# Feed-forwards that open token-major, a ring of ten weight units, and loads moved to the SyncE queue

## The chip, the cores and the metric

The kernel runs on one core of a Trainium2 chip. The metric is the device time of one execution in microseconds; the time before is the median of three executions. PE is TensorE, ACT ScalarE, DVE VectorE, POOL GpSimd, SP SyncE.

## The reference

Three transformer blocks run one after the other over 256 tokens of width 1024, and everything is float32. What matters here is the shape of one block:

```
h = h + rms_norm(mixer(rms_norm(h, n0)), n1)
h = h + rms_norm(ffn(rms_norm(h, n2)), n3)
conv_ffn: u, v = split(y @ w_up);  c = b + sum_j conv_w[j] * shift(u, j);  (gelu(c) * v) @ w_down
```

Block 0 has the even mixer (window attention and a gated recurrence), block 1 the odd mixer (attention with relative bias, 16 heads). The third block has three attention branches, one norm ahead of them and one ahead of its feed-forward, silu(gate) * up in place of the convolution, and no norm behind its products. The hidden width of a feed-forward is 2816, that is 22 column tiles of 128 features. Each column tile of a feed-forward has two halves: u (or gate) and v (or up).

## The kernel before, in words

**Split precision.** Each float32 operand is used as a rounded part `hi` and a rest `lo`; a product is three matmuls (hi·hi, hi·lo, lo·hi). Weights arrive as 346 *units* of 128x1024 floats (512 KB). SP loads a unit into slot n % 8 of `raw` as soon as the unit eight before it is used (`unit_used`, L399). ACT rounds it (`hi<-raw`, L500), DVE subtracts (`lo<-raw,hi`, L1148), PE waits for `lo_done`. ACT and DVE execute in program order, so the calls `units(upto)` between the other steps say when units are rounded and split.

**Two ways to multiply.** *Token-major* (`tokens_by`, matmuls on L788): 128 tokens of the activations are the stationary operand, 512 weight columns move; a unit holds 128 rows of the weights, and it takes six matmuls for each of the two token tiles. I call these six a *part*. *Feature-major* (`features_of`, L852): 128x128 weights are stationary and both token tiles move (256 columns); a unit holds all 1024 rows of 128 columns and takes 24 matmuls. It needs both token tiles of the activations from its first matmul on. The up-projection of each feed-forward is feature-major (44 units, `each_tile`, which is straight code for the first four tiles, a loop for sixteen, and straight code for two), and the down-projection is token-major (22 units).

**What stands between a projection and the next one.** The last `TAIL` = 6 units of a projection that ends in a norm run as a group: token tile 0 of all six, then token tile 1 of all six, so that tile 0 is normed while PE works on tile 1. `norms_between` (L540 on ACT, L1216 on DVE) does for each token tile: sum of squares of the product (ACT, L520), times gain (`weigh_product`, L1179), the root (POOL, L428 and L430), add into `h` (L1212), squares and gain again for the next norm (L520, L1179), root, `scale` (L1193). Then PE transposes the tile (`turn_normed`, eight transposes on L863), ACT copies the rounded part (`turned_hi`, L538) and DVE the rest (`turned_lo`, L1199). The transposes of tile 0 are put ahead of the last unit's part of tile 1 (L817). Those of tile 1 stand ahead of what follows: in a feed-forward ahead of its first matmul (`turn_normed(stage, base, 1)`, L1018), in a token-major projection ahead of the sixth unit of the leading group of six (`LEAD`, L809), which runs tile 0 first. There are five such boundaries between two projections: even_out to up0, down0 to odd_v, odd_out to up1, down1 to moba_qk, and merge_out to up2 (this one has no norm on the product). In the three that lead to an up-projection (`FEATURE_MAJOR`) no weight unit is split between the two products with the gain and `scale` of tile 1; in the other two, one is split ahead of `scale` and one behind it.

**Other loads.** POOL issues the gain rows (512 KB each, broadcast), twelve constants and sixteen bias tables from its own queue. SP issues the input `h`, the memory input and the weights.

Of the kernel before, what the change touches and what calls it, by code (L numbers as in the profile page):

```python
# [45 lines left out]
RAW = 8  # L46
# [5 lines left out]
    ("up0", 44, 8, 128), ("down0", 22, 1, 1024),  # L52
    ("odd_v", 8, 1, 1024), ("odd_qk", 16, 8, 128), ("odd_out", 8, 1, 1024),
    ("up1", 44, 8, 128), ("down1", 22, 1, 1024),
    ("moba_qk", 8, 1, 1024), ("both_v", 8, 1, 1024), ("fox_qk", 8, 1, 1024), ("mem_q", 8, 1, 520),
    ("gates", 24, 8, 128), ("branches", 12, 4, 256), ("merge_out", 8, 1, 1024),
    ("up2", 44, 8, 128), ("down2", 22, 1, 1024),
# [18 lines left out]
LEAD, TAIL = 6, 6  # L76
# [51 lines left out]
def lay_out(a):  # L128
# [8 lines left out]

    r = np.arange
# [6 lines left out]
    u += columns(a["ffn_w_up"][0], two) + rows(a["ffn_w_down"][0], r(D))  # L145
    u += rows(odd, r(2048, 3072)) + columns(odd, pairs) + rows(a["odd_w_out"][0], r(D))
    u += columns(a["ffn_w_up"][1], two) + rows(a["ffn_w_down"][1], r(D))
# [5 lines left out]
    u += columns(np.concatenate([a["w_gate_2"][0], a["w_up_2"][0]], 1), two) + rows(a["w_down_2"][0], r(D))  # L153
# [22 lines left out]
def build(nc, dram, out):  # L176
    with ExitStack() as ctx:
# [52 lines left out]
        nlf = sb("nlf", [NT, P])  # L230
# [48 lines left out]
        state = [s.rearrange("p (h e) -> p h e", h=HB) for s in state]  # L279
        qc_t = xhat[:, 0, :].rearrange("p (a b) -> p a b", a=4)  # L280
# [27 lines left out]
        conv_begun, conv_done, glued = sem("conv_begun"), sem("conv_done"), sem("glued")  # L308
        hmul, h_hi_done, h_lo_done = sem("hmul"), sem("h_hi_done"), sem("h_lo_done")
# [44 lines left out]
        def each_tile(engine, tile):  # L354

            for r in range(4):
                tile(0, r)
            with engine.Fori(1, KF // 4) as i:
                for r in range(4):
                    tile(i, r)  # L360
            for r in range(KF % 4):
                tile(KF // 4, r)

        def qk_place(j, f):

            if j == 0:
                return ps[:, 2 + f, 0:S]
            return ps[:, 6 + f, S * (j % 2):S * (j % 2) + S]

# [17 lines left out]
        def _(sp):  # L387

            sp.dma_start(mem_x[:, 0, :], dram["mem"][0:P, :]).then_inc(mem_in[0], 16)
            sp.dma_start(ident[:, :], dram["c_ident"]).then_inc(ident_in, 16)  # L390
            for n in range(RAW):
# [4 lines left out]
                sp.dma_start(raw[:, n, :], dram["weights"][n]).then_inc(raw_in[n], 16)  # L396
            with sp.Fori(0, UNITS // RAW - 1) as i:
                for s in range(RAW):
                    sp.wait_ge(unit_used, RAW * i + s + 1)  # L399
                    sp.dma_start(raw[:, s, :], dram["weights"][RAW * i + (RAW + s)]).then_inc(raw_in[s], 16)  # L400
            for n in range(UNITS - UNITS % RAW, UNITS):
                sp.wait_ge(unit_used, n - RAW + 1)
                sp.dma_start(raw[:, n % RAW, :], dram["weights"][n]).then_inc(raw_in[n % RAW], 16)
# [6 lines left out]
        def _(pool):  # L410
            def gain_load(g):
                if g >= 2:
                    pool.wait_ge(weighed, half_count(g - 2, 1, 1))
                pool.dma_start(gain[:, g % 2, :], dram["gains"][g:g + 1, :].partition_broadcast(P)).then_inc(gain_in[g % 2], 16)

            pool.memset(half[:, :], -0.5).then_inc(set_up, 1)
            gain_load(0)
            gain_load(1)
# [13 lines left out]
            def head_roots(i, nh, d):  # L432
# [7 lines left out]
            loads = [  # L440
                (rope_a[:, :, :, :].rearrange("p a t f -> p (a t f)"), dram["c_rope_a"]),
                (rope_m[:, :, :, :].rearrange("p a t f -> p (a t f)"), dram["c_rope_m"]),
                (window[:, :], dram["c_window"]), (causal[:, :], dram["c_causal"]),
                (block_causal[:, :], dram["c_block"]), (keep[:, :], dram["c_keep"]),
                (pick[:, :, :].rearrange("p a b -> p (a b)"), dram["c_pick"]),
                (conv[:, :, :, :].rearrange("p a b c -> p (a b c)"), dram["conv"]),
                (head_gain[:, :], dram["head_gains"].partition_broadcast(P)),
                (rows_in[:, :], dram["rows_in"].partition_broadcast(P)),
                (lb_in[:, :, :].rearrange("p a b -> p (a b)"), dram["lb"]),
                (hw[:, :], dram["hgrn_w"].partition_broadcast(P)),  # L450
            ]
            for dst, src in loads:
                pool.dma_start(dst, src).then_inc(const_in, 16)
            pool.memset(ones[:, :], 1.0).then_inc(set_up, 1)
            pool.memset(s_t[:, :, :, :], 0.0).then_inc(set_up, 1)
            pool.memset(nlf[:, :, :], 0.0).then_inc(set_up, 1)
            gain_load(2)
            gain_load(3)
# [10 lines left out]
            gain_load(4)  # L469
            gain_load(5)  # L470
            root(4, 5)
            gain_load(6)
            gain_load(7)

            pool.wait_ge(unit_used, last("down0"))
            for hh in range(16):
                if hh >= 4:
                    pool.wait_ge(row_max, ATT["c"][0] + hh - 3)
                pool.dma_start(bias[:, hh % 4, :], dram["rel"][hh]).then_inc(bias_in[hh % 4], 16)
            root(6, 7)  # L480
            gain_load(8)
            gain_load(9)
            root(8, 9)
            gain_load(10)
# [7 lines left out]
        def _(act):  # L492
            done = [0]

            def round_unit(n, s=None, q=None, w=None):

                s, q = (n % RAW, n // RAW) if s is None else (s, q)
                act.wait_ge(raw_in[s], 16 * (q + 1))
                w = WIDTH[n] if w is None else w
                act.activation(hi[:, s, :w], raw[:, s, :w], ACT.Copy).then_inc(hi_done, 1)  # L500

            def units(upto):
                loops = (upto - done[0]) // RAW
                if loops >= 2:
                    n = done[0]
                    with act.Fori(0, loops) as i:
                        for s in range(RAW):
                            round_unit(RAW * i + (n + s), (n + s) % RAW, i + (n + s) // RAW, UNIT)
                    done[0] += RAW * loops
# [30 lines left out]
            def norms_between(g, p, base, name, stage, turn_base):  # L540


                units(last(name) + 2)
# [8 lines left out]
                if stage not in FEATURE_MAJOR:  # L552
                    units(last(name) + 6)
# [18 lines left out]
            def feed_forward(layer):  # L572

                up = FIRST[f"up{layer}"]
                J0 = KF * layer

                def copy(j, r):
                    act.wait_ge(hmul, J0 + j + 1)
                    act.activation(h_hi[:, j, :], pt[:, r % 2, :S], ACT.Copy).then_inc(h_hi_done, 1)

                def tile(i, r):

                    j = 4 * i + r
                    n, m = 8 * i + (up + 2 * r), up + 2 * r + 4
                    act.wait_ge(unit_used, n + 2)
                    if layer < 2:
                        act.activation(sc[:, r % 2, :S], ps[:, r, :S], ACT.Identity, scale=conv[:, layer, j, 2:3],  # L587
# [1034 lines left out]
```

## Time and profile before

| | |
|---|---|
| time, median of 3 (lowest, highest) | 1190.43 us (1188.77, 1191.32) |
| the profiled execution's own time | 1188.9 us |
| its span, first to last instruction | 1187.1 us |
| PE busy | 1125.4 us, 95% |
| DVE, ACT, POOL busy | 714.5, 560.1, 76.4 us |
| mean granted clock of PE | 0.959 |
| the chain that ended last | PE 88%, DVE 4%, ACT 3%, DMA 2% |

A matmul row such as `286 ns` is longer than the distance to the next one, since matmuls are pipelined; the distance between starts is what a matmul costs. In a timeline row the first number is the start, the second the time that the merged instructions cover, and a bracket holds the idle time of that engine just before it and what ended it.

### The profile page before, as it was taken

Reading aid. Unit: us, or ns where it says so; the run is one execution under the profiler, and the core shown is the slowest. Engines: PE = TensorE matmul, PEld = TensorE weight load, DVE = VectorE, ACT = ScalarE, POOL = GpSimd, SP = SyncE. Lnnn points to the kernel's source line nnn. Section 1 sums busy time; section 2 is a strip of 40 time slices with the busy share of each in tenths; the row PEclk is TensorE's granted clock in tenths of the full one; section 3 lists DMA queues with packets and bytes.
Section 4 is the critical chain, followed back from the end, with each engine's and each line's share of the span. In section 5 each row is a group of like instructions: output and inputs, shape, how many; then the busy total and the mean of one; then the engine's idle time right before and its main releaser. Section 6 shows DMA issues by size and latency. Waiting matters only on the chain.

```text
span 1187.1 us, 19769 instructions
## 1 busy us (share of the span) xinstructions
PE 1125.4 (95%) x7452; PEld 1022.4 (86%) x7452; DVE 714.5 (60%) x1111; ACT 560.1 (47%) x917; POOL 76.4 (6%) x113
## 2 busy tenths in 40 slices
PE   5999996999999899869999998999999997999998
PEld 4898676999988799759999886888999987999986
DVE  5668445666664656555666646756555675555552
ACT  5544333555553454434555534446543733444541
POOL 3300001000000211010000001212000000000000
PEclk9999578999999999889999999999999998999999
DMA  7953014545554653145554544665333344545552
GB/s 292 309 192 123 1 36 164 190 179 177 189 189 155 239 168 143 66 163 160 179 188 182 185 170 159 230 199 175 110 107 108 147 143 156 190 178 179 190 191 77
DMA packets 53934, 195.24 MB, mean 164 GB/s; under 512 B 6272, under 2 KB 6464, under 8 KB 53872
## 3 DMA queue, kind: packets, MB, share of 16 engines
q1 hardware_dynamic: 50816, 184.64, 45.2%
q0 software_dynamic: 3056, 9.73, 2.5%
q8 instruction: 45, 0.74, 0.2%
q14 instruction: 17, 0.14, 0.1%
HBM read 193.29 MB, written 1.05 MB: 164 GB/s over the span
## 4 chain that ended last, share of the span: by engine, by line
PE 88%; DVE 4%; ACT 3%; DMA 2%; POOL 1%; issue 1%; SPq 0%; ACTq 0%; DVEq 0%
PE ps L852 46%; PE ps L788 31%; PE ps L936 3%; PE ps L913 3%; DMA raw<-in_weights 2%; DVE lo L1148 2%; PE ps L925 1%; PE ps L863 1%; ACT hi L500 1%; DVE y_lo L1199 1%; ACT pr L520 1%; POOL ms L428 1%; PE ps L882 1%; PE ps L990 0%; POOL rstd L430 0%
## 5 line engine op out<-in xcount | busy, mean ns | idle before, releaser
L1148 DVE TENSOR_TENSOR lo<-raw,hi 128x1024 fp32r<-128x1024 f32 (+2 forms) x346 | 409.7, 1204 | 115.1 <-ACT hi L500 114.3
L852 PE MATMUL ps<-y_hi,hi 128*128 128x256 f32 x1504 | 430.8, 286 | 2.0 <-DVE y_lo L1199 2.0
L852 PE MATMUL ps<-y_lo,hi 128*128 128x256 f32 x1504 | 428.1, 285 | 0.0
L852 PE MATMUL ps<-y_hi,lo 128*128 128x256 f32 x1504 | 428.0, 285 | 0.0
L500 ACT ACTIVATE hi<-raw 128x1024 fp32r<-128x1024 f32 (+2 forms) x346 | 350.2, 1036 | 123.3 <-DMA raw<-in_weights 115.5
L852 PEld LDWEIGHTS ps<-y_hi,hi 128*128 128x128 f32 x1504 | 291.1, 194 | 4.1 <-issue 3.7
L852 PEld LDWEIGHTS ps<-y_lo,hi 128*128 128x128 f32 x1504 | 291.1, 194 | 0.0
L852 PEld LDWEIGHTS ps<-y_hi,lo 128*128 128x128 f32 x1504 | 290.9, 193 | 0.0
L788 PE MATMUL ps<-hi,h_hi 128*128 128x512 f32 x328 | 102.8, 395 | 3.9 <-DVE h_lo L1199 2.5
L788 PE MATMUL ps<-hi,h_lo 128*128 128x512 f32 x328 | 102.5, 394 | 0.0
L788 PE MATMUL ps<-lo,h_hi 128*128 128x512 f32 x328 | 102.2, 393 | 0.0
L788 PE MATMUL ps<-hi,y_hi 128*128 128x512 f32 (+2 forms) x288 | 87.9, 386 | 6.1 <-DVE y_lo L1199 3.6
L788 PE MATMUL ps<-lo,y_hi 128*128 128x512 f32 (+2 forms) x288 | 86.3, 380 | 0.0
L788 PE MATMUL ps<-hi,y_lo 128*128 128x512 f32 (+2 forms) x288 | 86.2, 380 | 0.0
L587 ACT ACTIVATE sc<-ps,conv 128x256 f32<-128x256 f32 x44 | 24.8, 565 | 121.2 <-PE ps L852 121.2
L788 PEld LDWEIGHTS ps<-hi,h_hi 128*128 128x128 f32 x328 | 61.1, 189 | 18.2 <-DVE h_lo L1199 2.9
L788 PEld LDWEIGHTS ps<-hi,h_lo 128*128 128x128 f32 x328 | 61.9, 189 | 13.6
L1317 DVE SCALAR_TENSOR_TENSOR sc<-ps,conv,sc 128x255 f32<-128x255 f32 x44 | 21.2, 483 | 86.9 <-ACT sc L587 86.9
L788 PEld LDWEIGHTS ps<-lo,h_hi 128*128 128x128 f32 x328 | 61.9, 189 | 13.2
L788 PEld LDWEIGHTS ps<-hi,y_hi 128*128 128x128 f32 x288 | 52.8, 191 | 17.9 <-DVE y_lo L1199 5.3
L788 PEld LDWEIGHTS ps<-lo,y_hi 128*128 128x128 f32 x288 | 53.7, 190 | 10.5
L788 PEld LDWEIGHTS ps<-hi,y_lo 128*128 128x128 f32 x288 | 53.5, 190 | 10.5
(237 smaller groups left out, 974.1 us busy)
## 6 DMA issues: line engine op xcount, KB each, us to landing
raw<-in_weights SPq DMA_DIRECT2D x346, 512.0 KB, 3.5
gain<-in_gains POOLq DMA_DIRECT2D x11, 512.0 KB, 5.3
bias<-in_rel POOLq DMA_DIRECT2D x16, 128.0 KB, 2.9
mem_x<-in_mem SPq DMA_DIRECT2D x2, 512.0 KB, 7.1
h<-in_x SPq DMA_DIRECT2D x1, 1024.0 KB, 14.0
out<-h SPq DMA_DIRECT2D x2, 512.0 KB, 2.6
pick<-in_c_pick POOLq DMA_DIRECT2D x1, 512.0 KB, 6.0
head_gain<-in_head_gains POOLq DMA_DIRECT2D x1, 256.0 KB, 6.7
```

The costliest lines, as they stand in the source:

```text
L428: pool.tensor_scalar(ms[:, g % 2, t:t + 1], ss[:, g % 2, t, 0:1], ss[:, g % 2, t, 1:2], EPS, ALU.add, ALU.add).then_inc(scaled_ms, 1)
L500: act.activation(hi[:, s, :w], raw[:, s, :w], ACT.Copy).then_inc(hi_done, 1)
L520: act.activation(junk[t][:, i, :], halves[i], ACT.Square, scale=D ** -0.5, accum_out=ss[:, g % 2, t, i:i + 1]).then_inc(squared, 1)
L587: act.activation(sc[:, r % 2, :S], ps[:, r, :S], ACT.Identity, scale=conv[:, layer, j, 2:3], bias=conv[:, layer, j, 3:4]).then_inc(conv_be ...
L788: mm = pe.matmul(ps[:, base + 2 * t + half_, :cw], x[:, k, tok], w[:, n % RAW, c0:c0 + cw], start=first and k == 0, stop=final and n == la ...
L852: mm = pe.matmul(dst, w[:, s % RAW, at], x(k), start=first and k == 0, stop=final and k == nk - 1)
L863: mm = pe.transpose(ps[:, base + 2 * t + kh, kk * P:(kk + 1) * P], src[:, t, (4 * kh + kk) * P:(4 * kh + kk + 1) * P], ident[:, :])
L882: mm = pe.transpose(ps[:, b, kk * P:(kk + 1) * P], src[:, t, c0 + kk * P:c0 + (kk + 1) * P], ident[:, :])
L913: mm = pe.matmul(dst, q[:, t * P:(t + 1) * P], k[:, :n], start=True, stop=stage != "f")
L936: mm = pe.matmul(place(stage, hh, t), pt[:, a % 2, i * P:(i + 1) * P], v(kt), start=kt == 0, stop=kt == kts[-1])
L1148: dve.tensor_tensor(lo[:, s, :w], raw[:, s, :w], hi[:, s, :w].bitcast(F32), ALU.subtract).then_inc(lo_done, 1)
L1317: dve.scalar_tensor_tensor(c[:, 1:S], ps[:, r, 0:S - 1], conv[:, layer, j, 1:2], c[:, 1:S], ALU.mult, ALU.add).then_inc(dve_link, 1)
```

## The change

- The ring has ten slots (`RAW` 8 to 10). The groups at projection ends have seven units (`TAIL` 6 to 7). Three units of the next projection are split ahead of the first norm, where there were two. One of them is split ahead of `turned_lo` of tile 0, where there were two; one between that and the product of tile 1 with the gain; one ahead of `scale` of tile 1, now in all five boundaries. The transposes of tile 0 stand one part earlier.
- A feed-forward's first three column tiles (`lead0` to `lead2`, six half units each: 512 rows by 256 columns) are made token-major, all of token tile 0, then all of token tile 1. The transposes of token tile 1 of the activations stand ahead of the sixth half unit of token tile 0. The result is copied to `xhat` and turned to feature-major by twelve transposes, behind the first half of the fourth column tile.
- All loads are issued by SP, in one program order with the weights: gain 0 ahead of the first weights, gain 1 behind `x`, constants two at a time ahead of units 10 to 15, the other gains and the bias tables at fixed places. POOL issues none.
- No loops are left in the program of any engine. `nlf` lies in a part of `gate`; its memset on POOL stands later.

```diff
-RAW = 8
+RAW = 10
-LEAD, TAIL = 6, 6
+LEAD, TAIL, LEADS = 6, 7, 3
...
+        def ahead(j):
+            return 11 + j if j < 4 else 2 * j + 7
...
@@ SP
+            GAIN_AT = {FIRST["even_qf"]: (2, 3), FIRST["up0"] + 10: (4, 5), FIRST["odd_qk"] + 4: (6, 7), FIRST["up1"] + 10: (8, 9),
+                       FIRST["both_v"] + 6: (10,)}
+            gain_load(0)
+            for n in range(UNITS):
...
+                for g in GAIN_AT.get(n, ()):
+                    gain_load(g)
+                if n >= RAW:
+                    sp.wait_ge(unit_used, n - RAW + 1)
+                    for dst, src in loads[2 * (n - RAW):2 * (n - RAW) + 2]:
+                        sp.dma_start(dst, src).then_inc(const_in, 16)
+                for hh in BIAS_AT.get(n, ()):
+                    bias_load(hh)
+                sp.dma_start(raw[:, n % RAW, :], dram["weights"][n]).then_inc(raw_in[n % RAW], 16)
@@ ACT, feed_forward
+                act.wait_ge(lead_made, 2 * layer + 1)
+                act.activation(xhat[:, 0, 0:512], bank(0), ACT.Copy).then_inc(lead_copied, 1)
+                act.wait_ge(lead_made, 2 * layer + 2)
+                act.activation(xhat[:, 0, 512:768], lead_place(2, 0), ACT.Copy).then_inc(lead_copied, 1)
+                units(up + 10)
+                act.wait_ge(unit_used, up + 4)
+                act.activation(xhat[:, 1, 0:512], bank(2), ACT.Copy).then_inc(lead_copied, 1)
@@ PE
-                        if is_tail and n == last(name) - 1:
+                        if is_tail and n == last(name) - 2:
                             turn_next()
...
+                def lead(t):
+                    for j in range(LEADS):
+                        for half_ in range(2):
...
+                            if j == 0:
+                                pe.wait_ge(y_lo_done, 4 * stage + 2 * t + half_ + 1)
+                            if t == 0 and n == up + 2 * LEADS - 1:
+                                turn_normed(stage, base, 1)
+                            for kk in range(4):
+                                k, c = 4 * half_ + kk, slice(256 * kk, 256 * kk + 256)
+                                for x, w in ((y_hi, hi), (y_hi, lo), (y_lo, hi)):
+                                    mm = pe.matmul(lead_place(j, t), x[:, k, tok], w[:, n % RAW, c], ...)
...
+                lead(0)
+                lead(1)
+                column(3, 0)
+                pe.wait_ge(lead_copied, 4 * layer + 4)
+                for j in range(LEADS):
+                    turn_lead(j)
+                column(3, 1)
+                for j in range(4, KF):
+                    if j >= 8:
+                        pe.wait_ge(hmul, KF * layer + j - 3)
+                    column(j, 0)
+                    column(j, 1)
@@ DVE, norms_between
-                units(last(name) + 2)
+                units(last(name) + RAW - TAIL)
                 weigh_product(g, 0, base, tile_done, TAILS.index(name) + 1)
...
                 units(last(name) + 4)
                 turned_lo(stage, turn_base, y_lo, y_hi, (0,))
+                units(last(name) + 5)
                 weigh_product(g, 1, base, unit_used, last(name))
                 add_product(g, p, 1)
                 weigh(g + 1, 1, [h[:, 1, 0:512], h[:, 1, 512:D]])
-                if stage not in FEATURE_MAJOR:
-                    units(last(name) + 5)
+                units(last(name) + 6)
                 scale(g + 1, 1)
@@ DVE, feed_forward
+                units(up + 10)
+                dve.wait_ge(unit_used, up + 6)
+                dve.tensor_copy(xhat[:, 1, 512:768], lead_place(2, 1)).then_inc(lead_copied, 1)
+                for j in range(KF):
...
+                    units(up + ahead(j) - 1)
                     dve.wait_ge(glued, J0 + j + 1)
...
+                    units(up + ahead(j))
```

## Rows read from the trace of the kernel before

**Rows 1.** The page: granted clock and traffic in 40 slices of the span.
```profile
PEclk9999578999999999889999999999999998999999
...
GB/s 292 309 192 123 1 36 164 190 179 177 189 189 155 239 168 143 66 163 160 179 188 182 185 170 159 230 199 175 110 107 108 147 143 156 190 178 179 190 191 77
```

**Rows 2.** Who PE waited for over the span: us, times, longest.
```profile
PE ps L863 <- DVE xhat L1193: 33.5, 4, 10.4
...
PE ps L788 <- DVE lo L1148: 3.3, 3, 1.3
```

**Rows 3.** Busy time by stretch: length, PE, PEld, DVE, ACT, POOL, clock, DMA share, GB/s.
```profile
187.10:198.00 10.90, 2.05 (x9) 1.68 (x9) 7.09 (x13) 4.02 (x11) 3.17 (x6) 0.72 0.44 134
198.00:202.00 4.00, 4.00 (x19) 4.00 (x20) 0.61 (x1) 0.00 (x0) 0.00 (x0) 0.50 0.41 166
...
520.60:532.00 11.40, 1.99 (x9) 1.62 (x9) 7.59 (x13) 4.47 (x12) 3.17 (x6) 0.60 0.39 124
532.00:536.00 4.00, 4.00 (x19) 4.00 (x20) 0.69 (x1) 0.00 (x0) 0.00 (x0) 0.50 0.36 147
...
985.10:993.70 8.60, 2.04 (x9) 1.67 (x9) 6.48 (x11) 4.42 (x8) 1.13 (x2) 0.62 0.36 138
993.70:997.30 3.60, 3.60 (x17) 3.60 (x18) 0.64 (x1) 0.00 (x0) 0.00 (x0) 0.50 0.02 7
```

**Rows 4.** Timeline at the boundary from even_out to up0.
```profile
177.82 1.40 DVE L1179 TENSOR_TENSOR xhat<-ps,gain 128x512 f32<-128x512 f32 x2
...
186.46 0.63 PE L788 MATMUL ps<-hi,y_lo 128*128 128x512 f32 x2
...
187.36 1.28 DVE L1199 TENSOR_TENSOR y_lo<-ps,y_hi 128x512 fp32r<-128x512 f32 x2
...
188.56 1.28 DVE L1179 TENSOR_TENSOR xhat<-ps,gain 128x512 f32<-128x512 f32 x2
...
192.61 1.29 DVE L1179 TENSOR_TENSOR xhat<-h,gain 128x512 f32<-128x512 f32 x2
...
193.49 0.58 POOL L428 TENSOR_SCALAR ms<-ss 128x1 f32<-128x1 f32 x1 [2.43 <-ACT pr L520]
...
194.75 0.88 DVE L1193 TENSOR_SCALAR xhat<-xhat,rstd 128x512 f32<-128x512 f32 x2 [0.84 <-POOL rstd L430]
...
195.29 1.97 PE L863 MATMUL ps<-ident,xhat 128*128 128x128 f32 x8 [8.21 <-DVE xhat L1193]
```

**Rows 5.** Timeline at the boundary from down0 to odd_v.
```profile
389.53 0.73 PE L788 MATMUL ps<-hi,y_hi 128*128 128x512 f32 x2 [1.32 <-DVE y_lo L1199]
...
394.92 1.63 POOL L428 TENSOR_SCALAR ms<-ss 128x1 f32<-128x1 f32 x1 [2.43 <-ACT pr L520]
...
396.52 0.73 PE L788 MATMUL ps<-hi,y_hi 128*128 128x512 f32 x2 [1.26 <-DVE lo L1148]
...
399.30 1.09 PE L863 MATMUL ps<-ident,xhat 128*128 128x128 f32 x8 [1.12 <-DVE lo L1148]
```

**Rows 6.** The chain that ended last: start, us, what.
```profile
165.46 14.99 PE ps L788 x66
...
820.66 5.76 PE ps L852 x48
```

**Rows 7.** Timeline of the start, and of DVE near 46 us.
```profile
8.59 1.29 DVE L1179 TENSOR_TENSOR xhat<-mem_x,gain 128x512 f32<-128x512 f32 x2 [8.59 <-DMA gain<-in_gains]
...
14.84 1.22 PE L788 MATMUL ps<-hi,h_hi 128*128 128x512 f32 x2 [2.48 <-DVE h_lo L1199]
...
45.91 0.68 DVE L1245 TENSOR_REDUCE hs<-sc 128x4 f32<-128x512 f32 x1
```

**Rows 8.** Timeline of one column tile of up0 on ACT and DVE.
```profile
223.65 0.48 DVE L1317 SCALAR_TENSOR_TENSOR sc<-ps,conv,sc 128x255 f32<-128x255 f32 x1 [1.82 <-ACT sc L587]
...
224.77 0.40 ACT L594 ACTIVATE pr<-sc 128x256 f32<-128x256 f32 x1
224.90 1.22 DVE L1148 TENSOR_TENSOR lo<-raw,hi 128x1024 fp32r<-128x1024 f32 x1
```

More of the change, by code:

```diff
@@ L136, in columns, with up @@
         return [w[:, cols[c:c + width]].reshape(-1, P, width).transpose(1, 0, 2).reshape(P, -1) for c in range(0, len(cols), width)]
+    def up(w):
+        first = [x[:, c:c + UNIT] for x in columns(w, two[:LEADS * 256], 256) for c in (0, UNIT)]
+        return first + columns(w, two[LEADS * 256:])
     r = np.arange
@@ L352, in build @@
         junk = [sc, pr]
[L354 to L362, printed above, removed]
         def qk_place(j, f):
@@ L468, in _ @@
             root(2, 3)
-            gain_load(4)
-            gain_load(5)
             root(4, 5)
[L472 to L479, printed above, removed]
             root(6, 7)
-            gain_load(8)
-            gain_load(9)
+            pool.memset(nlf, 0.0).then_inc(set_up, 1)
             root(8, 9)
-            gain_load(10)
             for i in (4, 5, 6, 7):
@@ L493, in _, with round_unit @@
             done = [0]
[L495 to L499, printed above, removed]
+            def round_unit(n):
+                s, w = n % RAW, WIDTH[n]
+                act.wait_ge(raw_in[s], 16 * (n // RAW + 1))
                 act.activation(hi[:, s, :w], raw[:, s, :w], ACT.Copy).then_inc(hi_done, 1)
             def units(upto):
[L503 to L509, printed above, removed]
                 while done[0] < upto:
@@ L1029, in feed_forward @@
-                each_tile(pe, tile)
+                up = FIRST[f"lead{layer}"]
+                def lead(t):
+                    tok = slice(t * P, (t + 1) * P)
+                    for j in range(LEADS):
+                        for half_ in range(2):
+                            n = up + 2 * j + half_
+                            if t == 0:
+                                wait_unit(n)
+                            if j == 0:
[5 more added lines that the diff above has]
+                                for x, w in ((y_hi, hi), (y_hi, lo), (y_lo, hi)):
+                                    mm = pe.matmul(lead_place(j, t), x[:, k, tok], w[:, n % RAW, c],
+                                                   start=k == 0 and x is y_hi and w is hi, stop=k == KD - 1 and x is y_lo)
+                            if t == 1:
+                                mm.then_inc(unit_used, 1)
+                        if t == 0 and j >= 1:
+                            mm.then_inc(lead_made, 1)
@@ new lines, in turn_lead, with column @@
+                def turn_lead(j):
+                    for f in range(2):
+                        for t in range(NT):
+                            mm = pe.transpose(up_place(j, f)[:, t * P:(t + 1) * P], xhat[:, t, 256 * j + P * f:256 * j + P * f + P], ident[:, :])
+                    mm.then_inc(lead_turned, 1)
+                def column(j, f):
+                    n = up + 2 * j + f
+                    features_of(n, n % RAW, [up_place(j, f)], of_tiles(Y)).then_inc(unit_used, 1)
+                lead(0)
@@ L1224, in norms_between @@
                 turned_lo(stage, turn_base, y_lo, y_hi, (0,))
+                units(last(name) + 5)
                 weigh_product(g, 1, base, unit_used, last(name))
@@ L1589, in _ @@
             merged_low(1)
-            units(last("merge_out"))
+            units(last("merge_out") + RAW - TAIL)
             add_residual("merge_out", 4, 0)
```

185 lines of the change are left out of this document (77 added, 108 removed).

## The prediction, made before the changed kernel ran

> **What bounds the kernel now.** I read the page first: PE is busy for 95% of the span and carries the chain that ended last, so only what PE stands still for, or runs at a low clock for, can be won. [rows 1] show the clock lowest in the fifth to seventh slice (118 to 208 us) and dips at the 17th, 18th and 34th. Then the waits of PE: 33.5 us in four waits go to the normed activations, of which the longest, 10.4 us, is the start of the kernel [rows 2]. The other three, 23.1 us, are the openings of the three feed-forwards. The windows put numbers on them: the stretches from the last matmul of a projection to the first of the up-projection are 10.9, 11.4 and 8.6 us, with some 2 us of PE work in each (eight transposes), and behind each PE runs at clock 0.50, the level of 1.2 GHz, for 4.0, 4.0 and 3.6 us [rows 3]. The timeline says why: up0 needs both token tiles, and the norm of tile 1 can't begin before the last part of even_out [rows 4]. The opening of the token-major odd_v, which has tile 0 to work on, loses only 1.32, 1.26 and 1.12 us [rows 5].
>
> **Units used below.** A part (six token-major matmuls) takes 14.99 / 11 = 1.36 us; a feature-major matmul takes 5.76 / 48 = 0.12 us [rows 6], so one token tile of a lead half unit (12 matmuls of 256 columns) takes 1.44 us. I take the 256-column form in either layout as the same price: both load 128x128 and move 256 columns, and there are 24 for a unit before and after. A transpose takes 1.09 / 8 = 0.136 us at full clock [rows 5].
>
> **Feed-forward openings: what goes.** Stretches of 10.9 + 11.4 + 8.6 = 30.9 us. At full clock the 19, 19 and 17 matmuls behind them would take 2.28, 2.28 and 2.04 us, so the low clock costs 1.72 + 1.72 + 1.56 = 5.0 us. Together 35.9 us.
>
> **What comes back.** (1) The eight transposes of tile 1: 3 x 1.09 = 3.3 us. (2) Twelve transposes of the lead: 12 x 0.136 = 1.64 us, three times 4.9 us. Ends: 1.09 x 12/8 as taken, and at low clock 1.97 x 12/8 = 2.96 us each [rows 4], which would add 4.0 us; I take the first, as PE doesn't stand still ahead of them. (3) A rest of the wait for tile 1. Call E the end of the last part. For E, tile 0 must be turned: its chain takes from the product's end (177.82) until about 184.6 us, five parts, before and after the change, and y_lo of tile 0, now with one split (1.2 us) ahead of it instead of two and one part more of cover, is ready about 1 us before E; it was 1.5 us late (187.36 + 1.28 = 188.64 against E = 186.46 + 0.63 = 187.09). DVE then splits one unit and is free at E + 0.2. The chain of tile 1 runs 188.56 to 193.90 (5.34 us) up to the end of the second product with the gain; `scale` began 0.85 us later [rows 4]. Now a split stands between them. Where one stands there already, at odd_v, POOL's first root instruction took 1.63 us [rows 5] instead of 0.58 [rows 4], 1.05 us more, and `scale` waits for it: 0.85 + 1.05 = 1.9 us after the product. So the first normed half is there at E + 0.2 + 5.34 + 1.9 + 0.44 = E + 7.9. PE has five half units of lead until its transposes: 5 x 1.44 = 7.2 us. The wait is 0.7 us, twice 1.4 us. At up2 there is no norm on the product, the chain is shorter by over 2 us, and I take none. Ends for each opening: 0, and 2 us if DVE starts the chain as late as before (1.3 us more). Behind the transposes the sixth half unit (1.44 us) covers the copy of half a tile (about 0.6 + 0.7 us), so `lead(1)` waits for nothing.
>
> On the same rows, the Trainium skill, "SBUF — State Buffer", section "Who interferes with whom", says that a VectorE instruction with two inputs in SBUF keeps out a GpSimd instruction that reads SBUF. The split has two, and the trace agrees: 1.63 us with a split beside it, 0.58 without. It speaks against the change, since the split now stands there in the feed-forward boundaries as well. By it the wait is the 0.7 us above; without it `scale` would wait for the split alone and there would be nearly none.
>
> Net for the three: 35.9 - 3.3 - 4.9 - 1.4 = 26.3 us.
>
> **Openings of odd_v and moba_qk.** The wait for y_lo of tile 0 (1.32) goes, as above. The fifth unit's split now stands ahead of the tile-1 chain, so the wait for it (1.26) goes. What is late next is `scale`: PE reaches the transposes at E + 5 x 1.36 = 6.8 against E + 7.9, 1.1 us. So 3.70 becomes 1.1, and with the second, which repeats the pattern (the waits for the split in [rows 2] are three, two of them these), 5.2 us go. Ends: 1.4 (only the first wait goes each time, and half of that) and 7.4.
>
> **Start.** The first norm waited for gain 0 until 8.59 [rows 7], while gain 1 was moving beside it; now gain 1 comes behind `x`. At the 300 GB/s of the first slices [rows 1] a 512 KB load takes 1.7 us. In the one queue, gain 0 should land near 6.3, units 0 and 1 near 8.0 and 9.7; rounding, the copy of tile 0 and its rest put the first matmul near 12.8 instead of 14.84 [rows 7]. I take 1.9 us. Ends: 3, and -3 if `x` and gain 1 come late for the second norm. The constants come in the weights' queue up to unit 15. Adding up 12.9 MB at 300 to 320 GB/s they are complete near 43 to 45 us, and DVE wants them at 45.91 - 1.9 = 44.0 [rows 7]: 0 to 3 us of wait with little cover behind it, I take 0.5. Net 1.4 us.
>
> **The first tiles of the up-projections.** Behind the turned lead, tiles 0 to 3 get one split each. For a tile, DVE's cycle is from its first convolution step (223.65) to gelu's end (225.17), 1.52 us, then rounding 1.05, the split 1.22: about 3.8 us [rows 8]. The 15th unit is then split some 21 us after the first turned tile, with the table load of gelu (1.3 us) in it, and PE wants it 21.2 us after. So it just holds; I take 0.4 us in all, ends 0 and 3 us for each of two layers. Later tiles have two splits in about 4.2 us of DVE against 5.8 us of PE, so they catch up. Units 6 to 9 of an opening are split in the 9 us in which PE does `lead(1)`, and land before that at one unit in 1.7 to 2.3 us. The four copies of the lead are covered by `lead(1)` and the half column behind it (2.9 us).
>
> **Priced at nothing.** Groups of seven: no work is added, but PE comes to each unit of the group one part (1.36 us) earlier. In the down-projections the splits run ahead by the ring's depth, which hides it. In merge_out and odd_out, of eight units, the last four or two are split while PE works on the first; if that cover is gone it costs up to one split, 1.2 us, at each. I take none. Gains and bias tables in SP's order: each wait there is for something that is over when its turn comes, with nine units (over 25 us) queued ahead of the weights held back. Straight code instead of loops: the gates stage is straight code and does 48 matmuls in 5.76 us [rows 6], 0.1200 us each, and the loops run at the same within 0.001 us; over 2304 matmuls this is 0 to 2.3 us. POOL loses its DMA issues, which nobody waited for.
>
> **Sum.** 26.3 + 5.2 + 1.4 - 0.4 = 32.5 us. Against the profiled execution's 1188.9 us this is 1156.4; its time is 1.5 us under the median shown, so for the median 1158 us.
>
> **Rivals.**
> - *The openings are hidden, but the weights or the vector engine are late behind them* (15%): the 3.8 us cycle of the first four tiles is the thin place. At 4.5 us a tile it costs 4 x 0.7 = 2.8 us in layers 0 and 1, and with the start's gain lost as well, 2.8 x 2 + 1.4 = 7: 1165 us. For it: the margin is a few tenths. Against: DVE is idle for 1.82 us in each tile now [rows 8].
> - *Tile 1 isn't covered and the clock falls again* (8%): if the tile-1 chain starts late, PE waits 2 to 3 us at all five openings and the clock drops at the three feed-forwards (5.0 us): about 15 us back, 1173 us. Against: at odd_v waits of 1.3 us left the clock at full level.
> - *The change doesn't do what it says* (3%): lead(0) can't start before both tiles, because y_lo of tile 0 or the fourth and fifth units come with tile 1. Then 35.9 us stay and only the 5 us of the token-major openings and the start are left, less 4.9 us of transposes: 1189 us.
> - *Slower* (4%): fetching straight code. The loops of the up-projections hold 16 of 22 tiles; unrolled, 3 x 16 x 48 = 2304 matmuls and as many weight loads stream through PE's sequencer once each. From 32.5 / 2304 = 14 ns a matmul on (0.134 instead of 0.120 us) the gain is gone; at 20 ns, 1204 us. Against: the straight stages of the same density above. The Trainium skill, "Runtime: NRT & Kernel Launch", section "Instruction fetch mechanics", has it the other way round: a taken branch can stall the fetch, and straight code is preferred. By it there would be a gain here; the trace shows none to be had, as PE had no idle time in the loops.
>
> **How the numbers follow.** The forecast case has 70%, its own range is 1152 to 1163 us (the low end is all waits at nothing and 3 us at the start). To leave out no more than 2 in 10, the range reaches into the first rival: 1151 to 1168 us. Under 0.2% (2.4 us) a measurement of this kernel can't tell a change from none. Faster 0.94, same 0.02, slower 0.04.
>
> **What would show it.** Right: no wait of PE for the normed activations above 1.5 us after the start of the kernel, clock 1.00 over all openings, first matmul of the lead within 0.3 us of the group's end, twelve transposes in about 1.6 us, first matmul of the kernel near 12.8 us. Wrong: waits for `lo` in tiles 5 to 8 of an up-projection, a wait of DVE for constants over 3 us, gaps in long runs of matmuls that no semaphore explains, or a clock of 0.5 behind a boundary.

## The result, and the profile after

| | median us (lowest to highest, executions) | ratio to before, 95% |
|---|---|---|
| before, measured beside it | 1190.32 (1188.77 to 1191.32, 4) | |
| after | 1153.76 (1152.48 to 1154.90, 4) | 0.9696 [0.9683, 0.9709] |

36.6 us faster; forecast were 1158 and a range of 1151 to 1168. The two profiled executions are 1188.9 and 1154.57 us (spans 1187.1 and 1152.8), 34.3 apart, against a sum of 32.5. The other 2.2 us are where these two executions happened to lie in their own spreads: 1.4 under the median before, 0.8 over it after.

The page's slices of the granted clock and of the traffic, after:

```profile
PEclk9999569999999999899999999999999999999999
GB/s 326 313 194 146 1 19 139 259 184 182 185 186 150 214 208 151 79 133 245 184 183 184 192 135 206 229 213 148 129 102 103 145 130 215 186 184 184 187 193 37
```

The dips behind the three feed-forward boundaries are gone from the clock [rows 1]; those of the attention stages (fifth, sixth and seventeenth slice) stay. The waits of PE after, in total us, times, longest:

```profile
PE ps L859 <- DVE xhat L1213: 14.1, 5, 10.3
PE ps L784 <- DVE lo L1175: 1.6, 1, 1.6
PE ps L859 <- DVE y_lo L1219: 1.1, 2, 0.6
```

Before, 33.5 us in four waits [rows 2]. Now 10.3 are the start and 3.8 are shared by the four openings that have a product norm. No wait for `lo` is left but one at the start. Windows after, with PE busy first and its clock in the column behind POOL, of up0's opening, of the up-projection behind it, and of the openings of odd_v and moba_qk:

```profile
188.00:192.00 4.00, 4.00 (x36) 4.00 (x35) 2.73 (x5) 2.91 (x8) 0.86 (x2) 1.00 0.72 239
192.00:201.00 9.00, 8.25 (x71) 8.08 (x70) 5.88 (x9) 5.00 (x9) 2.19 (x2) 1.00 0.07 11
201.00:317.40 116.40, 116.40 (x973) 116.40 (x972) 79.85 (x124) 62.78 (x103) 0.00 (x0) 1.00 0.61 203
376.00:388.00 12.00, 10.87 (x54) 8.83 (x53) 8.96 (x13) 5.99 (x14) 3.06 (x4) 1.00 0.48 168
696.40:708.20 11.80, 10.68 (x52) 8.68 (x51) 8.86 (x13) 5.79 (x13) 3.06 (x4) 1.00 0.49 182
```

Where the windows of before had 2 us of PE work in 10.9 us and then clock 0.50 [rows 3], PE is now busy for all but 0.75 us of 188 to 201, at clock 1.00, and then without a gap for 116.4 us. The timeline of the same opening (start, us covered), the last part of even_out, the first lead matmul, and the chain of tile 1, to be laid beside [rows 4]:

```profile
186.95 0.61 PE L784 MATMUL ps<-hi,y_lo 128*128 128x512 f32 x2
187.41 0.28 PE L1028 MATMUL ps<-hi,y_hi 128*128 128x256 f32 x1
187.62 1.46 DVE L1199 TENSOR_TENSOR xhat<-ps,gain 128x512 f32<-128x512 f32 x2
...
189.19 0.30 POOL L461 TENSOR_SCALAR ms<-ss 128x1 f32<-128x1 f32 x1 [6.05 <-ACT pr L517]
...
192.56 1.63 POOL L461 TENSOR_SCALAR ms<-ss 128x1 f32<-128x1 f32 x1 [2.43 <-ACT pr L517]
192.89 1.22 DVE L1175 TENSOR_TENSOR lo<-raw,hi 128x1024 fp32r<-128x1024 f32 x1
194.28 0.56 POOL L463 TENSOR_TENSOR rstd<-ms,half 128x1 f32<-128x1 f32 x1
194.87 0.88 DVE L1213 TENSOR_SCALAR xhat<-xhat,rstd 128x512 f32<-128x512 f32 x2 [0.76 <-POOL rstd L463]
195.50 1.06 PE L859 MATMUL ps<-ident,xhat 128*128 128x128 f32 x8 [0.75 <-DVE xhat L1213]
```

The lead follows the last part without a gap, and POOL's root instruction takes 1.63 us beside the split. At 189.19 the same instruction takes 0.30 us, with DVE idle. So the 0.58 us of [rows 4] is more than its price alone: its first 0.4 us lie beside DVE's product with the gain. The chain that ended last, from there (start, us):

```profile
196.57 10.07 PE ps L1028 x84
206.64 2.88 PE ps L848 x24
209.52 1.31 PE ps L1038 x12
```

84 lead matmuls in 10.07 us are 0.1199 each, the price of the feature-major form [rows 6]; twelve transposes hold PE for 1.31 us. At up2, where no norm lies on the product, both turns stand in unbroken work:

```profile
955.34 0.87 PE ps L859 x8
956.21 2.75 PE ps L784 x12
958.97 7.20 PE ps L1028 x60
966.17 0.87 PE ps L859 x8
967.04 10.07 PE ps L1028 x84
```

### The profile page after: what moved, and what is told of

It is laid out like the page before. It is cut to its first block, busy times and chain, and to the rows that moved or that the text cites. A ratio compares the mean times of both kernels' runs of the same rounds, so it can differ in the third digit from the quotient of the medians.

```text
span 1152.8 us, 18024 instructions
## 1 busy us (share of the span) xinstructions
PE 1119.6 (97%) x7488; PEld 1020.2 (89%) x7488; DVE 716.0 (62%) x1114; ACT 558.5 (48%) x926; POOL 57.4 (5%) x74
## 4 chain that ended last, share of the span: by engine, by line
PE 90%; ACT 3%; DVE 3%; POOL 2%; issue 1%; DMA 1%; SPq 0%; ACTq 0%; DVEq 0%
PE ps L848 42%; PE ps L784 33%; PE ps L1028 3%; PE ps L932 3%; PE ps L909 3%; PE ps L859 2%; PE ps L921 2%; ACT pr L517 1%; POOL ms L461 1%; DVE lo L1175 1%; DMA raw<-in_weights 1%; POOL rstd L463 1%; PE ps L878 1%; ACT hi L504 1%; PE ps L986 1%
## 5 line engine op out<-in xcount | busy, mean ns | idle before, releaser
L848 PE MATMUL ps<-y_hi,hi 128*128 128x256 f32 x1360 | 387.2, 285 | 0.0
L848 PE MATMUL ps<-y_hi,lo 128*128 128x256 f32 x1360 | 384.8, 283 | 0.0
L848 PE MATMUL ps<-y_lo,hi 128*128 128x256 f32 x1360 | 384.8, 283 | 0.0
L504 ACT ACTIVATE hi<-raw 128x1024 fp32r<-128x1024 f32 (+2 forms) x346 | 346.5, 1036 | 76.4 <-DMA raw<-in_weights 76.2
L848 PEld LDWEIGHTS ps<-y_hi,hi 128*128 128x128 f32 x1360 | 260.7, 192 | 1.0 <-issue 0.7
L848 PEld LDWEIGHTS ps<-y_lo,hi 128*128 128x128 f32 x1360 | 260.7, 192 | 0.0
L848 PEld LDWEIGHTS ps<-y_hi,lo 128*128 128x128 f32 x1360 | 260.7, 192 | 0.0
L564 ACT ACTIVATE pr<-sc,neg 128x128 f32<-128x128 f32 x80 | 35.4, 445 | 49.4 <-DVE neg L1297 49.2
```

The source lines that it names most:

```text
L564: e = act.activation(pr[:, a % 2, c], src, ACT.Exp, bias=neg[:, col, t:t + 1], accum_out=tot[:, col, t:t + 1])
L848: mm = pe.matmul(dst, w[:, s % RAW, at], x(k), start=first and k == 0, stop=final and k == nk - 1)
```

## The experiments

Each edit is one to the kernel after, unless it says otherwise. "Before" of the batches was 1189.7, 1189.4 and 1189.3 us; the medians of different batches are compared only where the gap is several us.

### Which part of the change brings the time

**ring_only**: ring of ten, groups of seven, early turn, the new order of splits and SP's loads, without the lead (all columns feature-major, from the first on; the copies and turns of the lead go with it).

```diff
-("lead0", 6, 4, 256), ("up0", 38, 8, 128)
+("lead0", 0, 4, 256), ("up0", 44, 8, 128)      # lead1, lead2 alike
-LEAD, TAIL, LEADS = 6, 7, 3
+LEAD, TAIL, LEADS = 6, 7, 0
```

> The changed kernel without its token-major lead: the up-projections are feature-major from their first tile, as before; the ring of ten, groups of seven, the early transposes of tile 0 and SP's loads stay. Theory (the lead covers the norm of tile 1): each opening stands still again for the chain of tile 1. It starts some 1.3 us earlier than before and has the split ahead of scale (1.05 us), so the stretches are near 10.6, 10.6 and 7.5 us, with the clock at 0.50 for about 4 us behind each; against the changed kernel 25 us more, 1179 us. Rival (the deeper ring and the earlier transposes bring most of it): under 1165 us, with waits of PE for the normed activations of under 5 us at each feed-forward.

Measured 1178.78 (1178.00 to 1181.02), ratio 0.9915 [0.9889, 0.9941]. Its wait and one of its windows:

```profile
PE ps L852 <- DVE xhat L1201: 33.5, 6, 10.4
```

```profile
197.00:202.00 5.00, 4.75 (x25) 4.78 (x26) 0.80 (x2) 0.24 (x1) 0.00 (x0) 0.57 0.00 0
```

The 33.5 us stay, and so does the low clock behind them. The lead is worth 25 us of the 36.6; the rest of the change alone brings 11. By the starts of the same matmuls in the profiled executions of before and of ring_only, 6.2 of these 11 lie in the openings of odd_v and moba_qk, 2.8 in those of the three feed-forwards, and 1.6 in the odd mixer, where the clock is low for 6.9 us instead of 10.2.

**lead_only**: the lead and SP's loads, with ring, groups and turn as before. `RAW - TAIL` is also the number of units split ahead of the first norm: three after, two here and in ring8_early, four in groups_six.

```diff
-RAW = 10
+RAW = 8
-LEAD, TAIL, LEADS = 6, 7, 3
+LEAD, TAIL, LEADS = 6, 6, 3
-if is_tail and n == last(name) - 2:
+if is_tail and n == last(name) - 1:
```

> The lead kept, but a ring of eight, groups of six and the transposes of tile 0 ahead of the last part, as before. Theory: the lead brings most, and the ring's share is that DVE starts the chain of tile 1 on time: two splits stand ahead of y_lo of tile 0 again, so PE waits 1.3 us for it at an opening, and the tile-1 chain starts about 2.5 us later, some 3.2 us of waits at four openings instead of 0.9; 10 us more than the changed kernel, 1164 us. Rival (with eight slots the weights of the lead are late, as they arrive at one in 1.7 to 2.3 us against 1.44 us of use): waits for lo in every opening and over 1172 us.

Measured 1170.25 (1163.33 to 1172.27), ratio 0.9823 [0.9777, 0.9869]: 6 us above the theory. No opening waits for `lo`, so the rival is false. What came instead is the clock: it fell again behind the waits of odd_v, up1, moba_qk and up2:

```profile
390.90:394.30 3.40, 3.20 (x12) 2.94 (x13) 1.73 (x4) 1.82 (x3) 0.00 (x0) 0.50 0.00 0
524.00:527.40 3.40, 3.40 (x19) 3.40 (x18) 1.29 (x2) 2.06 (x5) 0.00 (x0) 0.50 0.00 0
718.50:721.90 3.40, 3.40 (x13) 2.92 (x12) 1.86 (x3) 2.65 (x4) 0.00 (x0) 0.51 0.00 0
974.50:977.90 3.40, 3.40 (x18) 3.40 (x18) 3.37 (x6) 1.33 (x4) 1.01 (x1) 0.51 0.08 34
```

Four times 3.4 us at half the clock cost up to 6.8 us, the size of the miss. At up0 the clock stayed, with waits of 2.0 us for `xhat` and 0.9 for y_lo, where up1 has 2.0 and 1.4. Its one execution at 1163.3 us, 7 us under the others, had a mean clock of 0.975 against their 0.968 to 0.969; 0.7% of 1168 us is 8 us. That execution has no trace, so that the four drops are what it lacks is inferred from its mean clock. Together with ring_only this shows an interaction: 11 and 19.5 us alone, 36.6 together, 6 more than the sum (which counts twice what both runs share, SP's loads). The trace of after has no such drop, so the clock is large enough for all of the 6; that is argued from sizes, no run separates it.

**turn_late**: the turn of tile 0 one part later.

```diff
-if is_tail and n == last(name) - 2:
+if is_tail and n == last(name) - 1:
```

> Only the place of tile 0's transposes goes back to one part before the end; ring and groups stay. Theory (DVE's order sets the tile-1 chain): y_lo of tile 0 ends 1.4 us later, the split behind it too, the chain of tile 1 starts 1.4 us later, and PE's wait at the transposes of tile 1 grows from 0.8 to 1.1 us to 2.2 to 2.5 us at four openings: 5.5 us more, 1159 us. Rival (there is slack between the two): same time as the changed kernel within 1 us.

Measured 1159.79 (1158.42 to 1162.10), ratio 0.9751 [0.9723, 0.9779]. Its wait row:

```profile
PE ps L859 <- DVE xhat L1213: 19.7, 5, 10.4
```

5.5 us more waiting than after (9.3 against 3.8 without the start), about one part (1.36) at each of four openings, and 6.0 to 6.3 us more time. Tile 0 is turned a part later, so ACT and DVE finish with it a part later and start the chain of tile 1 later: at up0 DVE's product of tile 1 starts at 188.65, 1.6 us behind the group's end at 187.06, where after has 0.2. The four waits are 2.1, 2.5, 2.1 and 2.5 us long. Behind the one at odd_v the clock was 0.51 from 390.2 to 393.7, some 1.7 us of time; behind the other 2.5 us, at moba_qk, and behind the two of 2.1 it stayed at full level.

**groups_six** and **ring8_early** divide the rest.

```diff
-LEAD, TAIL, LEADS = 6, 7, 3
+LEAD, TAIL, LEADS = 6, 6, 3      # groups_six; ring8_early has RAW = 8 besides
```

> After with groups of six instead of seven at the projection ends, ring of ten and all else kept. It divides what lead_only lost between ring and groups. Theory: the group's length is what counts, since it sets how long TensorE works on the second token tile while VectorE weighs and scales the first: one part of a unit (6 matmuls of 0.24, 1.44 us) is missing at each of five ends, less the slack of about 0.75, so 3 to 4 us: 1157 us, and the ring is then worth the other 7. Rival: the ring counts for nothing here, and groups_six comes out as slow as ring8_early, 1162 or more.

> After with the ring of eight half units and groups of six, the turn two parts before the end and everything else of the change kept: the run lead_only with the early turn. Theory: the early turn is worth what turn_late lost, 6.3 us, whatever the ring: 1164 us. What then still lies above after (10.5 us) belongs to ring and groups alone, as waits of TensorE for xhat and y_lo in the openings. Rival: with groups of six the early turn waits for VectorE itself and brings under 2 us: 1168 to 1170.

groups_six: 1160.27 (1158.52 to 1160.93), ratio 0.9753 [0.9740, 0.9766], 6.8 us above the repeat of after (1153.46), twice what I expected. The waits, and the place in question in even_out's group:

```profile
PE ps L859 <- DVE xhat L1213: 20.3, 9, 10.7
```

```profile
186.04 0.88 DVE L1213 TENSOR_SCALAR xhat<-xhat,rstd 128x512 f32<-128x512 f32 x2 [0.86 <-POOL rstd L463]
186.59 1.10 PE L859 MATMUL ps<-ident,xhat 128*128 128x128 f32 x8 [1.44 <-DVE xhat L1213]
```

Nine waits instead of five. The chain over tile 0 runs from 179.81 to the first normed half at 186.48, 6.7 us. Five parts (6.8 us) just cover it, four (5.4) don't: PE stands for 1.44 us ahead of the early turn at each of four ends, 5.8 us, and that is most of the 6.8. I had counted a slack of 0.75 that isn't there.

ring8_early: 1171.38 (1164.92 to 1173.34), ratio 0.9830 [0.9805, 0.9855], where the theory had 1164 and the rival 1168 to 1170. It isn't faster than lead_only (1170.25): with groups of six the early turn waits, as just shown. The fastest execution of each, 1164.92 and 1163.33, says the same. The rival holds: the early turn brings nothing in groups of six. What groups of seven bring without the early turn no run shows. Its chain ahead of tile 1's norm at up0, and the turn at its end:

```profile
182.12 4.62 DMA raw<-in_weights
...
186.76 1.07 ACT hi L504
...
187.85 1.23 DVE lo L1175
189.08 1.20 DVE y_lo L1219 x2
190.28 1.13 DVE lo L1175
191.41 0.61 DVE xhat L1199
```

```profile
199.21 1.06 PE L859 MATMUL ps<-ident,xhat 128*128 128x128 f32 x8 [1.91 <-DVE xhat L1213]
```

A slot that comes free late means a load that lands late (4.62 us from its issue), and its rounding and split stand in DVE's order ahead of y_lo and of tile 1's product. The first lead matmul, which marks the group's end, is at 189.95 here and tile 1's product at 191.33, 1.4 us behind it; after, these are 187.41 and 187.62, 0.2 apart. The 1.2 us come out as wait: 1.91 instead of groups_six's 0.75 at up0, and in all 24.9 us of waits for `xhat` (10.8 at the start) against 20.3 (10.7). So of the 11.1 us between ring8_early and groups_six, 4.5 are these waits, 1.1 a new wait of the lead for y_lo, and most of the rest the clock, 0.969 against 0.973 in the mean, 0.4% or nearly 5 us: at up0, odd_v, up1 and moba_qk it was at half for 3.4 us each, in groups_six at none of them. What two more slots cure is the lateness of DVE's queue; in ring8_early, behind the start, TensorE itself never waited for a split unit.

### What is left in the openings

**after_again** repeats the kernel after beside the next three: 1153.46 (1153.17 to 1155.33), ratio 0.9701 [0.9686, 0.9715].

> The changed kernel itself, beside the next three on the same chip: 1153 to 1155 us.

**split_late**: the sixth unit's split behind `scale` of tile 1, at all five boundaries.

```diff
-units(last(name) + 6)
 scale(g + 1, 1)
+units(last(name) + 6)
```

> In the changed kernel, DVE's split ahead of scale of tile 1 stands behind scale, at all five openings. Theory (the split's second SBUF input keeps POOL's root instruction out): that instruction takes 0.6 us instead of 1.63, scale starts 0.85 us behind the product with the gain instead of 1.9, and PE's wait at the transposes of tile 1 falls to nearly 0; the split, now 0.2 to 0.6 us late for the sixth unit, takes back a part: about 2 us less in all, 1152 us. Rival (the long root instruction has another cause): it stays at 1.6 us, scale doesn't move, the split comes 1.2 us later still, and the kernel is up to 4 us slower.

Measured 1153.99 (1152.80 to 1155.32): no gain. The trace at up0:

```profile
186.83 0.30 POOL L461 TENSOR_SCALAR ms<-ss 128x1 f32<-128x1 f32 x1 [6.05 <-ACT pr L517]
190.21 0.58 POOL L461 TENSOR_SCALAR ms<-ss 128x1 f32<-128x1 f32 x1 [2.43 <-ACT pr L517]
191.47 0.88 DVE L1213 TENSOR_SCALAR xhat<-xhat,rstd 128x512 f32<-128x512 f32 x2 [0.84 <-POOL rstd L463]
193.54 1.09 PE L859 MATMUL ps<-ident,xhat 128*128 128x128 f32 x8 [1.12 <-DVE lo L1175]
```

POOL's instruction is back at 0.58 us and `scale` is 1.04 us earlier in its chain (4.64 us behind the 186.83 row, against 5.68 behind 189.19 after). But PE's program has `wait_unit(n)` of the sixth unit ahead of the turn, so the turn now waits 1.12 us for a split that it doesn't use, where it waited 0.75 (5.3 us in four openings, 3.8 after). The stall only changed its name, which I had overlooked.

**turn_first**: split_late, and the turn of tile 1 ahead of that wait in PE's program.

```diff
+if t == 0 and n == up + 2 * LEADS - 1:
+    turn_normed(stage, base, 1)
 if t == 0:
     wait_unit(n)
 if j == 0:
     pe.wait_ge(y_lo_done, ...)
-if t == 0 and n == up + 2 * LEADS - 1:
-    turn_normed(stage, base, 1)
```

(and the same in `by_tile`, for odd_v and moba_qk)

> After, with the sixth opening unit's split behind VectorE's scale (as in the run split_late) and, in TensorE's program, the turn of the second token tile ahead of the wait for that unit instead of behind it. Theory: in the run split_late the scale came 3.4 us earlier at up0 and the turn then waited 1.12 us for a split that it does not need, only because the wait for the unit stood ahead of it (5.3 us in four openings). With the turn first it starts at the scale's end (about 192.5 at up0), lasts 1.06 and covers the 1.2 us split: waits of L859 for xhat in the four openings fall from 3.8 to under 1, waits for lo under 1; 1150 us, 3.6 less than after. Rival: some other part of the opening (tokens' low halves, the feature side) is as late, a new wait of about 1 us appears in each opening, and the time stays at 1153 to 1154.

Measured 1151.04 (1150.27 to 1151.65), ratio 0.9677 [0.9664, 0.9691]: 2.4 us under after_again, of the 3.6 expected. (The "3.4 us earlier" in that text compared absolute times of two executions with different starts; behind the same event it is 1.04.) Waits for `xhat` are left at the start alone:

```profile
PE ps L861 <- DVE xhat L1215: 9.7, 1, 9.7
PE ps L784 <- DVE lo L1177: 2.5, 3, 1.6
PE ps L1030 <- DVE lo L1177: 0.5, 2, 0.3
```

1.4 us of waits for the split remain (0.9 in the token-major openings, 0.5 in the leads): of the 3.8, 2.4 are gone. That the median says 2.4 too is in part chance. Between the starts of the same matmuls in the profiled executions, each of the four openings is only 0.4 us shorter than in after_again, 1.7 us in all. Another 1.5 us come from the odd mixer, where the clock is 0.50 from 475.7 to 482.6 and in after_again from 474.7 to 485.0, and 0.8 us are lost ahead of up0. The short stretch stands in seven of the thirteen profiles, split_late's and ring_only's among them, and the long one in before and after; what decides between them stays open.

### The start

**memset_late**: POOL's two set-up fills behind the sixth unit. **plain_gain**: the gains stored 128 times in memory, so that their loads are plain.

```diff
+pool.wait_ge(unit_used, 6)
 pool.memset(ones[:, :], 1.0).then_inc(set_up, 1)
```

```diff
-sp.dma_start(gain[:, g % 2, :], dram["gains"][g:g + 1, :].partition_broadcast(P))
+sp.dma_start(gain[:, g % 2, :], dram["gains"][g])
```

> In the changed kernel, POOL's two memsets behind the first roots (ones, s_t) wait until six units are used, near 35 us. Theory: in the changed kernel they run beside DVE's scale of the second norm, which took 1.72 us for its two halves instead of 0.87, and PE waited 1.63 us for the split behind it instead of 0.78. Without that, scale takes 0.87 us and all behind it is 0.85 us earlier: 0.85 us less. Rival (scale is slow by the load traffic of that time): no change.

> In the changed kernel, the gain rows lie 128 times in DRAM, and each gain load is a plain 128-row transfer instead of a broadcast of one row. Theory (a broadcast load takes the queue for some 4 us, not 1.7): gain 0 landed at 8.46 although nothing ran beside it, while the memory input landed 3.5 us after its issue and the two units behind it within 1.3 us of each other. Plain, gain 0 lands near 6, unit 0 near 7.3, the first matmul is near 11.8 instead of 13.9: 2 us less. Rival (the queue is slow to start whatever it moves): gain 0 still lands past 8, no change.

memset_late 1152.89 (1151.30 to 1153.72), plain_gain 1153.38 (1152.31 to 1154.24), beside after_again's 1153.46: neither can be told from it in the median. After, in the start, and then the same instruction in memset_late:

```profile
26.52 0.31 POOL L473 MEMSET ones<- 128x256 f32 x1
26.68 1.72 DVE L1213 TENSOR_SCALAR xhat<-xhat,rstd 128x512 f32<-128x512 f32 x2
26.78 0.95 POOL L474 MEMSET s_t<- 128x1024 f32 x1
```

```profile
26.78 0.87 DVE L1214 TENSOR_SCALAR xhat<-xhat,rstd 128x512 f32<-128x512 f32 x2
```

The scale takes twice as long beside the fills, and this is shown: each profile with the fills there has it (1.33 us for the first half, 0.47 for the second), and PE then waits 1.6 us for the split behind it, in before, memset_late and best 0.8. plain_gain's trace had gain 0 at 6.92 us where after's had it at 8.46, and I first took that for the price of the broadcast. The other traces forbid it. Gain 0 landed, in the ten profiles of after and its variants with broadcast loads, at 6.69, 6.93, 7.83, 8.12, 8.46, 8.58, 8.59, 8.84, 8.96 and 9.02 us, and without broadcast at 6.92 and 7.47 (the run best). The start varies by 2.3 us from one execution to the next with the same loads in the same order, and two values within that spread settle nothing. Whether the broadcast costs time stays open.

**best**: turn_first, memset_late and plain_gain together.

> The edits of turn_first, memset_late (POOL's two set-up fills after the sixth unit) and plain_gain (gains replicated in DRAM, loaded without a broadcast) together. Theory: they touch different stretches and add up: 3.6 in the openings, 0.6 to 0.9 by the fills, and by the trace of plain_gain 1.7 at the start, of which its median showed 0.1: 1147 to 1149.5 us. Rival: the openings give nothing, 1152 to 1153.

Measured 1149.87 (1149.26 to 1150.78), ratio 0.9668 [0.9655, 0.9682]: the fastest version, 3.6 us (0.3%) under after_again, 1.2 under turn_first, and a little above the 1147 to 1149.5 expected, which had counted 1.7 us for the gains.

## Why the prediction was right, step by step

The checkpoints (start of the same instruction in both profiled executions) give each term its size:

| term | forecast us | profiled pair us |
|---|---|---|
| opening of up0 | -9.2 | -9.8 |
| opening of up1 | -9.7 | -10.8 |
| opening of up2 | -7.4 | -8.0 |
| openings of odd_v and moba_qk | -5.2 | -6.3 |
| start | -1.4 | +0.5 |
| first tiles of the up-projections | +0.4 | 0 |
| sum | -32.5 | -34.3 |

The sum is better than its terms: the openings gave 3.4 us more than forecast and the start 1.9 us less, and that these partly cancel is luck.

- **The stretch and the low clock go: right.** The windows show it for up0, and ring_only shows that nothing else in the change does it.
- **Rest of the wait for tile 1: right, mechanism and size.** Forecast 0.7 at up0 and at up1, 1.1 at the token-major openings, none at up2: 3.6 us in all. Measured 3.8 in four waits, 0.75 at up0. The product starts 0.2 us behind the first lead matmul (187.62 and 187.41), and POOL takes 1.63 us beside the split, as the prediction had it. The Trainium skill, "SBUF — State Buffer", section "Who interferes with whom", says that a VectorE instruction with two inputs in SBUF keeps out a GpSimd instruction that reads SBUF; the trace agrees (1.63 against 0.58 us in split_late). What it was worth only showed once PE's order was mended too, in turn_first: 1.7 us in the four openings.
- **Openings of odd_v and moba_qk: waits right, size short by 1.1.** Their waits went from 3.7 and 3.6 us to 1.1 each, as forecast. But PE now stops once where it stopped three times, and a stop costs more than its wait: at the first one before, the starts are 387.81, 389.53 and 389.87, 1.7 and 0.34 us apart where unbroken work has 0.23 twice, which makes 1.6 us for a wait of 1.32. Two stops of 0.3 at each opening make the 1.1.
- **Transposes: dear by a fifth.** Twelve take 1.31 us of PE, 0.109 each, and eight 0.87 in unbroken work; I took 0.136 from eight behind a wait. That is 0.33 and, where nothing is waited for, 0.22 us an opening. The low clock before was also worth more than the windows of [rows 3] held: it lasted for 20, 22 and 18 matmuls in 4.19, 4.62 and 3.77 us, that is 1.8, 2.0 and 1.6 us above 0.12 each, where I took 1.72, 1.72 and 1.56. Another 0.2 us of up0's row lies in the stages ahead of its opening, and 0.4 us of up1's in the odd mixer. With these the three rows come out within 0.2 us.
- **Start: failed.** The step "gain 0 should land near 6.3" took the load's bytes over the mean bandwidth as its time. It landed at 8.46 in the profiled execution and at 8.5 in the median of ten, about where it was before (8.59) with gain 1 beside it. Units 0 and 1 did gain from the queue: the first matmul stands 5.5 us behind gain 0 instead of 6.25, at 13.93. Then 1.3 us were lost again: behind gain 0's landing the fifth unit's matmuls began after 20.7 us before, 21.2 after, 19.9 in memset_late. 0.8 of it goes to a step that the prediction priced at nothing, "POOL loses its DMA issues, which nobody waited for". Before, twelve of these issues (26.99 to 33.5 us) stood ahead of POOL's fills and kept them away from the second norm. Another 0.45 us is lost among the first 18 matmuls: eight of the distances between their starts are 0.43 us after and five before, where the later ones are 0.23.
- **Catching up, constants and straight code: no cost seen.** 888 feature-major matmuls follow the turned lead in 106.55 us, 0.1200 each, unbroken. DVE's cycle in the first tiles of up0 is 3.57 us, where I had 3.8. DVE waits for no constant. So the first rival and the slower one, which needed 0.134 us for each matmul, are both false.
- **The clock falling again**: not in after, but it was nearer than 8% suggests. lead_only and ring8_early have the waits of 2 us that this rival named, and six of their nine executions came out 6 to 9 us above the fastest of their kernel.
- **Priced at nothing, and worth much**: "Groups of seven: no work is added". I entered groups, ring and early turn only as conditions of the coverage. Without them 16.5 us are missing (lead_only), some 7 of them by the clock. They were right inside the forecast (five parts for tile 0's chain, one split ahead of y_lo) and never stood in the text as a price.

## What to carry to other kernels

When a chain on the side engines is to be hidden behind matmuls, count it in units of the matmul work that is issued meanwhile: here 6.7 us needed five parts of 1.36 us, and four left PE standing at four boundaries. A stall that is taken away upstream comes back under another name if the waiting engine's program has another wait ahead of the instruction that was freed, so read both orders before moving one. And a start that jitters by 2 us between executions can't be judged from two traces; line the events up behind a common one, and look at all the profiles that share the code.

## What the runs showed of the hardware that I had not expected

- A fill on POOL slows VectorE: two 128x512 multiplications by a per-partition scalar took 1.72 us beside MEMSETs of 128x256 and 128x1024 and 0.87 us without. The first, which started while the fills ran, took 1.33 us, the second 0.47.
- POOL's instruction on 128x1 took 0.30 us with VectorE idle, 0.58 with a two-input product of VectorE over its first 0.4 us, and 1.63 with the product and the split behind it.
- The token-major form with 256 columns and the feature-major one cost PE the same, 0.1199 and 0.1200 us for each matmul.
- Waits of equal length leave the clock at full speed once and lower it another time: in the one trace of turn_late, 2.5 us at odd_v were followed by 3.5 us at 0.51, and 2.5 us at moba_qk by full clock. The executions of lead_only differ in the same way: 1163.3 us with a mean clock of 0.975, and 1170 to 1172 us with 0.968 to 0.969.
- The first gain load landed between 6.69 and 9.02 us in ten profiled executions with the same loads ahead of it.
